# ScalarE instead of SP issues the loads of value pages, two pages a step

## The reference

```
k_past = cache_k[e][page_table].reshape(Bs, past, H_DIFF, 2 * DH_DIFF)
v_past = cache_v[e][page_table].reshape(Bs, past, H_DIFF, DV_DIFF)
s = einsum('bqhmd,bkhmd->bhmqk', q, k) * scale
p = softmax(s);  a = p[:, :, 0] - lam * p[:, :, 1];  o = einsum('bhqk,bkhe->bqhe', a, v)
```

## Time and profile before

| | us |
|---|---|
| median of 3 runs | 2200.06 |
| lowest and highest | 2194.59, 2203.40 |
| the profiled execution | 2195.29 |
| its span | 2193.5 |
| TensorE busy in the span | 1888.4 |
| VectorE busy | 996.0 |
| GpSimd busy | 635.1 |
| ScalarE busy | 540.3 |

### The profile page before, as it was taken

The page is one execution under the profiler, slowest core; times in us unless marked ns, Lnnn a source line. Parts: engine busy times, 40 slices in busy tenths (PEclk is TensorE's granted clock), DMA queues, the critical chain, the costliest instruction groups (busy, mean ns, idle before and its releaser), DMA issues.

```text
span 2193.5 us, 35957 instructions
## 1 busy us (share of the span) xinstructions
PE 1888.4 (86%) x14217; PEld 1713.2 (78%) x14217; DVE 996.0 (45%) x1400; ACT 540.3 (25%) x822; POOL 635.1 (29%) x519
## 2 busy tenths in 40 slices
PE   5855778666756687999999999997999999999998
PEld 5753545444544446999999999987999999999998
DVE  2696676954654434443234333338332344323421
ACT  4321122221111202322122223330322323212211
POOL 1366352554565300133023110002311413301400
PEclk8976767878777888999999999997999999999999
DMA  7144664677877772232223222220232322323231
GB/s 225 60 149 146 206 210 155 207 252 244 270 244 258 246 250 97 87 96 87 96 87 96 94 92 77 75 68 14 74 100 87 96 92 83 101 92 89 86 104 59
DMA packets 218304, 288.05 MB, mean 131 GB/s; under 512 B 12993, under 2 KB 149778, under 8 KB 217890
## 3 DMA queue, kind: packets, MB, share of 16 engines
q1 hardware_dynamic: 215306, 281.95, 39.7%
q0 software_dynamic: 656, 1.51, 0.4%
q10 hardware_dynamic: 2208, 2.75, 0.4%
HBM read 274.96 MB, written 11.21 MB: 130 GB/s over the span
## 4 chain that ended last, share of the span: by engine, by line
PE 68%; DVE 11%; issue 7%; DMA 5%; SPq 3%; POOL 3%; ACT 2%; ACTq 0%; DVEq 0%; POOLq 0%
PE ps L1604 17%; PE ps L1606 17%; PE ps L1605 16%; PE ps L1425 4%; PE ps L1427 4%; PE ps L1426 4%; DMA vbuf<-in_cache_v 3%; POOL kbuf L636 3%; DVE Sc L1112 2%; SPq L498 2%; PE ps L1460 2%; DMA kbuf<-in_cache_k 1%; SPq L497 1%; PE ps L1671 1%; DVE w_lo L487 1%
## 5 line engine op out<-in xcount | busy, mean ns | idle before, releaser
L487 DVE TENSOR_TENSOR w_lo<-raw,w_hi 128x1024 fp32r<-128x1024 f32 x238 | 335.7, 1418 | 509.0 <-ACT w_hi L480 507.7
L636 POOL TENSOR_TENSOR kbuf<-kbuf,Qb 128x512 f32<-128x512 f32 x256 | 338.5, 1349 | 217.5 <-DMA kbuf<-in_cache_k 161.0
L1604 PE MATMUL ps<-xg_hi,w_hi 128*128 128x260 f32 x1408 | 399.6, 284 | 0.5 <-DVE sTs L1380 0.5
L1606 PE MATMUL ps<-xg_hi,w_lo 128*128 128x260 f32 x1408 | 399.4, 284 | 0.0
L1605 PE MATMUL ps<-xg_lo,w_hi 128*128 128x260 f32 x1408 | 398.2, 283 | 0.0
L1425 PE MATMUL ps<-w_hi,xg_hi 128*128 128x256 f32 (+1 forms) x1200 | 370.6, 309 | 14.8 <-DVE w_lo L487 6.4
L480 ACT ACTIVATE w_hi<-raw 128x1024 fp32r<-128x1024 f32 x248 | 258.7, 1052 | 458.3 <-PE ps L1606 411.3
L1426 PE MATMUL ps<-w_lo,xg_hi 128*128 128x256 f32 (+1 forms) x1200 | 360.8, 301 | 0.0
L1427 PE MATMUL ps<-w_hi,xg_lo 128*128 128x256 f32 (+1 forms) x1200 | 359.5, 300 | 0.0
L1604 PE MATMUL ps<-h_hi,w_hi 128*128 128x260 f32 x1024 | 289.7, 283 | 0.0
L1606 PE MATMUL ps<-h_hi,w_lo 128*128 128x260 f32 x1024 | 289.6, 283 | 0.0
(11 more groups left out here) (266 smaller groups left out, 2579.7 us busy)
## 6 DMA issues: line engine op xcount, KB each, us to landing
kbuf<-in_cache_k SPq DMA_DIRECT2D x256, 256.0 KB, 3.8
vbuf<-in_cache_v SPq DMA_DIRECT2D x256, 256.0 KB, 3.4
raw<-in_w_ffn_up SPq DMA_DIRECT2D x64, 512.0 KB, 3.9
raw<-in_w_ffn_down SPq DMA_DIRECT2D x64, 512.0 KB, 3.4
raw<-in_w_in_odd SPq DMA_DIRECT2D x48, 512.0 KB, 3.8
raw<-in_w_in_even SPq DMA_DIRECT2D x36, 512.0 KB, 5.4
raw<-in_w_out_odd SPq DMA_DIRECT2D x24, 512.0 KB, 3.4
raw<-in_w_out_even SPq DMA_DIRECT2D x12, 512.0 KB, 3.4
```

Of the source, the lines that this page charges most:

```text
L487: dve.tensor_tensor(w_lo[:, c.slot], raw[:, c.slot % 2], w_hi[:, c.slot].bitcast(F32), ALU.subtract).then_inc(lo_made, 1)
L636: pool.tensor_tensor(kk, kk, Qb[:, s % 2, :], ALU.mult).then_inc(k_weighed, 1)
L1604: pe.matmul(out, wh, xh, start=kk == 0, stop=False, skip_group_check=True)
L1606: mm_ = pe.matmul(out, wl, xh, start=False, stop=kk == KC * groups - 1, skip_group_check=True)
```

## The change

ScalarE issues the value pages. `kv_step` makes a new step kind, `VL`, in each j of the value range: quad n+1's pages 0 and 1 in the j of V step n, pages 2 and 3 in the next j. The first quads, which SP loaded among the keys, are loaded by ScalarE between `rstd_made` and its first evacuation, the second of them after it has waited for `x_saved` and `xg_lo_made`. SP keeps everything else. Waits, buffers, semaphores and the pages themselves are the same.

```
 def kv_step(j):
     ...
     n, part = divmod(PER * (j - LAG), QUAD)
-    if 0 <= n < NQ and part == 0:
-        out.append(("V", n))
+    if 0 <= n < NQ:
+        if part == 0:
+            out.append(("V", n))
+        if n > 0:
+            out.append(("VL", n - 1 + Q_SLOTS, part // PER))
...
-        def values_in(eng, n):
+        def values_in(eng, n, half):
             if n < NQ:
                 wait(eng, v_used, n - Q_SLOTS + 1)
-                for j in range(QUAD):
+                for j in range(PER * half, PER * half + PER):
                     page(eng, vbuf[n % Q_SLOTS][:, j, :], cache_v, QUAD * n + j, v_loaded[n % Q_SLOTS])
...
 # SP, ahead of its loop
-            for n in range(LOW_QUADS):
-                values_in(sp, n)
...
-            for n in range(LOW_QUADS, Q_SLOTS):
-                values_in(sp, n)
...
 # SP, in its loop
-                        if step[0] == "V" and step[1] > 0:
-                            values_in(sp, step[1] - 1 + Q_SLOTS)
...
 # ScalarE, among its steps
+                elif kind == "VL":
+                    values_in(act, i, step[2])
...
 # ScalarE, ahead of its loop
             act.wait_ge(rstd_made, 1)
+            act.wait_ge(pt_loaded, 16)
+            for n in range(LOW_QUADS):
+                for half in range(QUAD // PER):
+                    values_in(act, n, half)
+            act.wait_ge(x_saved, 16)
+            act.wait_ge(xg_lo_made, KD)
+            for n in range(LOW_QUADS, Q_SLOTS):
+                for half in range(QUAD // PER):
+                    values_in(act, n, half)
             for m in range(N_IN + 1):
```

## The result

| | before | after |
|---|---|---|
| median, us | 2201.72 (4 runs) | 2168.81 (4 runs) |
| lowest and highest | 2194.59, 2203.40 | 2164.26, 2173.62 |
| span of the profiled execution | 2193.5 | 2162.5 |

The ratio is 0.9857, 95% interval 0.9823 to 0.9891: the change makes the kernel faster by 1.4%, 33 us. The forecast was 77 us less (2118). The time lies inside the stated range and moved the way that was forecast.

The account below looks back on a forecast made before the run. TensorE was held between 186 and 832 us by value loads late in SP's queue, 165 us of waits. 2195.3 - 38 (second stretch) - 40 (first) - 6 (third) + 7 (start) = 2118 us, range 2062 to 2186.

Parts of the forecast that it names:

- part 1: SP's queue: 256 value loads leave, key loads delayed 3.2 us a slot less; the order matters, not SP's time.
- Part 2: ScalarE's issues: 0.85 us a page, 3.4 us a slot, covered by its waits up to 1.9 us in the second stretch.
- Part 3: ScalarE's added wait for `v_used` of the quad before: it never stands, cost 0.
- Part 4: Load chain from ScalarE's evacuation: 7.9 us fits a slot of 6.1 or more, so value waits go nearly everywhere save behind softmax.
- Part 5: Second stretch: 38 us off (278 to 240), lower end 12; four softmax places keep waits, about 3 us each comes back.
- Part 6: First stretch: 40 us off, VectorE then busy at 0.85; ends 12 and 59.
- Part 7: Third stretch: value quads no longer queue behind SP's state loads, 6 us off; ends 0 and 9.
- Part 8: Start: eight loads and the `x_saved` wait delay ScalarE's first evacuation, a loss of 7 us; ends 3 and 12.
- Rival 1: ScalarE's in-order queue up to 744 us becomes the bound from 1.9 us a page: 2243 us, slower; chance 0.11.
- Rival 2: Shared DMA transfers bind; keys and values collide and waits shift to the keys: 2192 us, no change; chance 0.08.
- Rival 3: GpSimd's 9-key ring and VectorE's scoring take over and hold TensorE: 2163 us; chance 0.12.
- Rival 4: More than the waits: with fewer pauses TensorE's clock rises to 0.85 and its work shrinks: 2084 us; chance 0.13.

Follow-up runs that it names:

- e4: Kernel before, SP still issuing all loads, but in each slot the value loads stand ahead of the key loads: 2147.6 us, ratio 0.9751.
- e13: Changed kernel, ScalarE issuing each whole quad right behind the value step that frees its buffer, ahead of the softmax steps: 2132.7 us, ratio 0.9682.
- e1: Changed kernel, but ScalarE issues all four value pages in the slot's first step: 2158.3 us, ratio 0.9798.
- e5: Kernel before, GpSimd copying each partition's maxima instead of the all-reduce over partitions (result not the reference's): 2157.0 us, ratio 0.9811.
- e6: e3 with GpSimd copying each partition's maxima instead of the all-reduce over partitions: 2118.0 us, ratio 0.9636.
- e9: Changed kernel, whole quads issued by ScalarE right behind the value step freeing their buffer, first two quads issued by SP: 2122.4 us, ratio 0.9640.
- e12: e3 with five of the six VectorE instructions of each retention rotation left out (result not the reference's): 2137.1 us, ratio 0.9722.
- e3: Changed kernel, with whole quads issued in the slot's first step and the first two quads issued by SP: 2153.3 us, ratio 0.9791.
- e8: Changed kernel with one more register load a page on ScalarE, absent from the trace, so effectively the changed kernel again: 2176.6 us, ratio 0.9897.
- e2: Changed kernel, but SP issues the first two quads as before, ahead of ScalarE's loop: 2173.1 us, ratio 0.9862.
- e7: e3 with value pages behind the first two quads loaded to half their columns, same number of loads: 2135.4 us, ratio 0.9709.
- e14: Changed kernel, but SP issues whole quads right behind the value step freeing their buffer, behind the step's keys: 2134.9 us, ratio 0.9710.

## Why the prediction was wrong in size

*What bounds, and part 1: right.* The value loads were late by their place in SP's queue. e4 moves nothing but the place and gains 53 us.

*Part 2, ScalarE's issues: right.* 2.79 to 2.88 us for four pages, where 3.4 were forecast; a register load takes 0.281 us and the issue 0.344. The cover holds: between the first 97 us and the end of the attention TensorE stands 1.6 us in all for an evacuation (L781). *Part 3, the wait for `v_used`:* no ScalarE wait on TensorE's value step shows at the issues.

*Part 4 failed: "So the value wait goes nearly everywhere, save behind the softmax".* The chain itself was sized well. From the end of the last issue to the landing I took 4 us; worked out over value steps 2 to 60 the median is 4.4 us and one in ten is over 6.7 (before: 3.4 and 4.7), so the chain is 7.8 us as a rule, as forecast (7.9), and 10 us in the slow tenth. What failed is "It fits a slot of 6.1 us or more", held against the mean slot of 9.3 us, or 8 after the change. The mean has the waits themselves in it, which were to go. Measured from one value step's start to the next, less the wait at the second, the 30 slots of the second stretch had a median of 5.9 us before, and 16 of them were under 6.1. In the changed kernel 18 of the 30 are under 6.1 us and 16 of these end in a value wait; of the 12 longer ones, 2 do. The value waits of the first two stretches are 121 us, where under 50 was the sign of being right. So the bound of 6.1 us was right, and more than half of the slots are below it; the trace of the kernel before had shown that.

Behind it stands the place of the loads: the change issues a quad one slot later than its buffer allows. I took that place as given, and its lead as ample. e13 makes the lead 3 us longer and keeps the quads whole; it gives 36 of the 44 us that are missing, some 26 by the lead and 10 by the whole quads, the latter little more than the scatter between jobs.

*Part 5 failed at the softmax: "about 3 us each comes back".* I had seen that half of the quad stands behind ScalarE's wait, and priced it as a gain. SP had issued the quad ahead of the softmax, 3.1 us before the exponential at step 31; ScalarE issues the second half behind it, and the two pages then still need their issue and landing, so the five waits grew from 40 to 66 us instead of shrinking to about 25. e1 shows the queueing, but also that freeing it returns only 11 us, while the waits a step later grow. That GpSimd's pause around the all-reduce holds TensorE there too is likely, as the reduction costs 35 to 45 us (e5, e6), but not shown for these steps. The cap that I took from the transfers, 240 us for the stretch at a share of 0.90, was no bad one: e9 reaches 240.3, at 0.85.

*Part 6, the first stretch: over-sized, 40 forecast, 17 measured.* Its value steps waited 27 us less, but TensorE's idle time in the stretch fell by 6 us only: the wait that ends the stretch, at step 23, grew by 7, and waits for tiles of VectorE and ScalarE by 13 (rqT at L1401 from 5.3 to 13.1 us, pq at L1514 from 5.6 to 8.1). The other 11 of the 17 us are TensorE's busy time. Its premise that VectorE's busy time stays was wrong as well: 206 us became 223 for the same instructions. The rotation's are longer, since more of them run while GpSimd multiplies keys. Over the six rotation lines, 74 us became 83. First before, then after, VectorE's groups of two of the six, one of them the line that grew most:

```profile
L1074 DVE TENSOR_TENSOR stg<-stg,cst 128x256 f32<-128x256 f32 x20 | 15.2, 760 | 0.7
L1072 DVE TENSOR_TENSOR swp<-stg,cst 128x128 f32<-128x128 f32 x20 | 11.0, 552 | 0.0
```

```profile
L1082 DVE TENSOR_TENSOR stg<-stg,cst 128x256 f32<-128x256 f32 x20 | 17.2, 861 | 0.7
L1080 DVE TENSOR_TENSOR swp<-stg,cst 128x128 f32<-128x128 f32 x20 | 15.4, 768 | 0.0
```

With the loads early enough (e13) this stretch is 244.5 us, VectorE busy for 88% of it; e12, built on e3, shows that VectorE's work is on the path of this stretch.

*Part 7, the third stretch: the number came out, 6 us forecast and 5.4 measured, but by luck.* The value waits that were to go are still there, 8.8 us for 9.2. From value step 53 to 63 the profile before took 75.1 us, the changed kernel's 70.4, and the same program in e8 77.6: the gain is smaller than this scatter. *Part 8, the start:* forecast +7, in the profile +9.6 to the first value step. Whether it reaches the end differs: e2 against the changed kernel and e3 against e1 show nothing, e9 against e13 10 us, with intervals that overlap. That it is absorbed where a later wait follows anyway is likely, but not shown.

*The sum.* With the parts as measured: -17.2 - 18.0 - 5.4 + 9.6 = -31.0, where -77 stood. The place of the loads (part 4) makes some 26 us of the difference and the split around the softmax (part 5) some 10.

*The rivals.* Rival 1 is refuted by the trace: ScalarE's pages are 0.81 us apart, far from 1.9, and TensorE hardly waits for an evacuation; e8, meant to test it, did not. Rival 2, transfers bind: halving the bytes of values is worth some 18 us (e7), so it is not the whole. "Issuing engines are not separate DMA queues" ("DMA: Bandwidth & Descriptors" of the Trainium skill) states the sharing that e7 shows, keys landing 1.1 us sooner when value bytes go; by the rule alone e9, with all bytes and issues as before, should have gained nothing, and it gained 77 us. Rival 3 came nearest in number (2163), but its mechanism, the key ring in place of the value wait, is not what happened: value waits themselves stayed. Something of its kind lies beneath: once e13 takes the value waits away, 65 us of waits for VectorE's and ScalarE's tiles take their place. Rival 4: the clock rose as it said, from 0.75 to 0.78 and from 0.79 to 0.83, and with it TensorE's busy time fell by 11 us in each stretch, which is part of the 17 and 18 us rather than on top of them. The idle time alone gave 13 us.

The best version run is e9, 2122.4 us, 3.6% under the kernel before.

## What to carry to other kernels

When a load is late, ask for two points of time and not for one: when its buffer comes free, and when the queue that issues it gets there; the distance between them is the most that an edit can win, and it need not win that: in e13 94 us of value waits went and 36 us of time. A new place in the same queue may do it: e4 and e14 gain 53 and 66 us with SP alone, where the move to ScalarE gave 33. Moving loads to another engine moves them behind that engine's waits: list these before, and don't split a group of loads around one. Hold the chain of a load against each slot and not against the mean slot, and take the waits that you mean to remove out of the slots first.

## What the runs showed of the hardware

- ScalarE issues a page as cheaply as SP: register load 0.281 us beside 0.267, issue 0.344 beside 0.333, four pages in 2.8 us from either.
- With two queues issuing, landings were longer: values 3.4 to 4.2 us and keys 3.8 to 4.4 us by the change alone, at a DMA share that rose only from 0.78 to 0.79 in the second stretch. In e14, where one queue issues everything at the early place, they are 3.6 and 4.0 us, at 2135 us.
- An elementwise VectorE instruction with two inputs in SBUF takes 0.43 us with none of GpSimd's beside it (L1074 of the kernel before: 0.424 to 0.429 in 10 of 20), and 1.37 to 1.41 us in 7 of the 10 cases that overlap one. L1072, 0.28 us alone, takes 1.35 to 1.38 us then: both last about as long as one of GpSimd's multiplies, 1.28 us at the median. In the changed kernel such long ones rose from 7 to 9 and from 5 to 9 of 20 on these two lines; the six rotation lines cost 9 of the 16 us by which VectorE's busy time grew in the first stretch.
